# Attentions of a two-block model on one NeuronCore: maxima taken scaled and negated, scores issued one step further ahead

## What is computed

```python
s = jnp.einsum('bqhd,bkhd->bhqk', qb, k).astype(jnp.float32) * scale
s = jnp.where(key_pos[None, :] <= q_pos[:, None], s, -jnp.inf)
p = jax.nn.softmax(s, axis=-1)
if mix is not None:
    p = mix(p)                      # diff_branch: p of head 2h minus lam * p of head 2h+1
return jnp.einsum('bhqk,bkhd->bqhd', p.astype(v.dtype), v)
```

## Time and profile before

| | |
|---|---|
| median of 3 executions | 4144.8 us (4137.83 to 4156.16) |
| the profiled execution | 4138.23 us, its span 4136.4 us |
| busy, share of the span | PE 93%, PEld 78%, DVE 40%, ACT 35%, POOL 34% |
| granted TensorE clock, mean | 0.973 |

### The profile page before, as it was taken

The page is one execution under the profiler, slowest core; times in us unless marked ns, Lnnn a source line. Parts: engine busy times, 40 slices in busy tenths (PEclk is TensorE's granted clock), DMA queues, the critical chain, the costliest instruction groups (busy, mean ns, idle before and its releaser), DMA issues. The chain is left out here.

```text
span 4136.4 us, 57230 instructions
## 1 busy us (share of the span) xinstructions
PE 3854.7 (93%) x23428; PEld 3229.0 (78%) x23428; DVE 1670.0 (40%) x3370; ACT 1430.4 (35%) x2322; POOL 1414.1 (34%) x525
## 2 busy tenths in 40 slices
PE   6998989999989899999989989999999888889999
PEld 5766878887876678788769967888888777867887
DVE  5845152322384524332261464311124676754111
ACT  3434242342234423333232364211122544433221
POOL 2211323343321132234322322223222567643342
PEclk8899999999999999999999999999999999999999
DMA  3221414434222142344412211112222111103332
GB/s 116 56 83 40 139 54 141 122 118 127 76 56 83 39 130 64 120 119 142 127 51 72 75 25 32 51 52 76 62 57 71 43 42 52 41 17 88 91 98 74
DMA packets 476080, 323.18 MB, mean 78 GB/s; under 512 B 31449, under 2 KB 472236, under 8 KB 475820
## 3 DMA queue, kind: packets, MB, share of 16 engines
q1 hardware_dynamic: 422112, 268.18, 22.5%
q10 hardware_dynamic: 53708, 51.33, 3.7%
HBM read 315.74 MB, written 2.16 MB: 77 GB/s over the span
## 5 line engine op out<-in xcount | busy, mean ns | idle before, releaser
L96 POOL TENSOR_TENSOR w_lo<-w_raw,w_hi 128x2048 fp32r<-128x2048 f32 (+6 forms) x329 | 1157.5, 3523 | 2417.8 <-ACT w_hi L228 2417.4
L228 ACT ACTIVATE w_hi<-w_raw 128x2048 fp32r<-128x2048 f32 (+3 forms) x278 | 471.9, 1698 | 1113.8 <-PE psum L264 1068.2
L262 PE MATMUL psum<-xF_hi,w_hi 128*128 128x512 f32 x1232 | 493.3, 400 | 15.7 <-ACT a_relud L1673 6.8
L264 PE MATMUL psum<-xF_hi,w_lo 128*128 128x512 f32 x1232 | 484.3, 393 | 0.0
L263 PE MATMUL psum<-xF_lo,w_hi 128*128 128x512 f32 x1232 | 480.7, 390 | 0.0
L262 PE MATMUL psum<-ffn_h_hi,w_hi 128*128 128x512 f32 (+1 forms) x1056 | 376.5, 357 | 2.2 <-issue 1.3
L264 PE MATMUL psum<-ffn_h_hi,w_lo 128*128 128x512 f32 (+1 forms) x1056 | 375.0, 355 | 0.0
L263 PE MATMUL psum<-ffn_h_lo,w_hi 128*128 128x512 f32 (+1 forms) x1056 | 373.7, 354 | 0.0
L262 PEld LDWEIGHTS psum<-xF_hi,w_hi 128*128 128x128 f32 x1232 | 232.6, 189 | 69.9 <-ACT a_relud L1673 8.4
L264 PEld LDWEIGHTS psum<-xF_hi,w_lo 128*128 128x128 f32 x1232 | 232.1, 188 | 53.8
L263 PEld LDWEIGHTS psum<-xF_lo,w_hi 128*128 128x128 f32 x1232 | 232.2, 189 | 48.7
(11 more groups left out here) (554 smaller groups left out, 8183.4 us busy)
## 6 DMA issues: line engine op xcount, KB each, us to landing
w_raw<-in_w_in_dram SPq DMA_DIRECT2D x56, 1024.0 KB, 5.2
ada_w<-in_ada_w_dram ACTq DMA_DIRECT2D x48, 1024.0 KB, 6.9
w_raw<-in_ffn_w_in_dram SPq DMA_DIRECT2D x88, 512.0 KB, 5.1
w_raw<-in_w_in_dram SPq DMA_DIRECT2D x78, 512.0 KB, 4.2
w_raw<-in_ffn_w_out_dram SPq DMA_DIRECT2D x32, 704.0 KB, 4.6
w_raw<-in_w_branch_dram SPq DMA_DIRECT2D x74, 256.0 KB, 4.6
w_raw<-in_hg_w_in_dram SPq DMA_DIRECT2D x32, 512.0 KB, 4.8
w_raw<-in_na_w_qkv_dram SPq DMA_DIRECT2D x12, 1024.0 KB, 5.1
```

Of the source, the lines that this page charges most:

```text
L96: return eng.tensor_tensor(pair.lo, src, pair.hi.bitcast(F32), ALU.subtract)
L228: act.activation(self.w(j).hi, self.raw_w(j), ACT.Copy).then_inc(*self.high_done.up(1))
L262: pe.matmul(out, left.hi, right.hi, start=first, stop=False)
L264: return pe.matmul(out, left.lo, right.hi, start=False, stop=last)
```

## The change

H gives the scaled and negated maximum straight away: the fused operation multiplies by -scale and reduces with min, into `bias`, and writes the masked scores already multiplied by -scale; the exponential then takes `scale=-1.0`. The `tensor_scalar` behind it, its wait, and the tile `top` of `paired_attention` are gone. Without mask and with scale 1.0 (`na`) `tensor_reduce` runs with `negate=True`; `mem` keeps both operations. The exponential of a unit is released by its own unit, where it was released by the step.

In `attention` the loops are written anew: PE issues T(s-1), S(s+1), F(s-2); DVE issues H(s+1), R(s-2), I(s-1); ACT issues c(s-1), e(s+1), and `raise_part` after them. `paired_attention` keeps its order.

```diff
                 C.enter(pe)
+                scores(0)
                 for s in range(NU // 2 + 2):
-                    if s < NU // 2:
-                        scores(s)
                     turn(s - 1)
+                    if s + 1 < NU // 2:
+                        scores(s + 1)
                     if features:
                         feature_sums(s - 2)
...
                     if mask is None:
-                        step(dve.tensor_reduce(column(top, u), scores_at(u)[:, 0:N], AX.X, ALU.max))
+                        if scale == 1.0:
+                            dve.tensor_reduce(column(bias, u), scores_at(u)[:, 0:N], AX.X, ALU.max, negate=True).then_inc(*max_found.up(1))
+                        else:
+                            step(dve.tensor_reduce(column(top, u), scores_at(u)[:, 0:N], AX.X, ALU.max))
+                            dve.tensor_scalar(column(bias, u), column(top, u), -scale, None, ALU.mult).then_inc(*max_found.up(1))
                     else:
...
-                        step(dve.tensor_tensor_reduce(dst, src, mask, 1.0, -3.0e38, ALU.add, ALU.max, column(top, u)))
-                    if not features:
-                        dve.tensor_scalar(column(bias, u), column(top, u), -scale, None, ALU.mult).then_inc(*max_found.up(1))
-                    elif u % 2:
-                        dve.tensor_scalar(columns(bias, u // 2), columns(top, u // 2), -scale, None, ALU.mult).then_inc(*max_found.up(2))
+                        dve.tensor_tensor_reduce(dst, src, mask, -scale, 3.0e38, ALU.add, ALU.min,
+                                                 column(bias, u)).then_inc(*max_found.up(1))
...
                 C.enter(dve)
-                for s in range(NU // 2 + 2):
-                    for u in group(s):
+                for s in range(-1, NU // 2 + 2):
+                    for u in group(s - 1):
+                        if u in dve_copies:
+                            copy(u)
+                    for u in group(s + 1):
                         highest(u)
...
                 C.enter(act)
-                for s in range(NU // 2 + 1):
-                    for u in group(s):
-                        N = width(u)
...
+                for s in range(-1, NU // 2 + 1):
                     for u in group(s - 1):
...
+                    for u in group(s + 1):
+                        N = width(u)
+                        act.wait_ge(*max_found.at(u + 1))
+                        if u >= 4:
+                            act.wait_ge(*turned.at(u - 3))
+                        src, by = (scores_at(u)[:, 0:N], scale) if units[u]["mask"] is None else (probs[u % 4][:, 0:N], -1.0)
+                        act.activation(probs[u % 4][:, 0:N], src, ACT.Exp, bias=column(bias, u), scale=by,
+                                       accum_out=column(den, u)).then_inc(*exped.up(1))
```

`paired_attention` has the same edit of its fused operation and its exponential:

```diff
-                    step(dve.tensor_tensor_reduce(probs[:, u % 6, 0:N], scores_at(u)[:, 0:N], units[u]["mask"], 1.0, -3.0e38,
-                                                  ALU.add, ALU.max, column(top, u)))
-                    dve.tensor_scalar(column(bias, u), column(top, u), -scale, None, ALU.mult).then_inc(*max_found.up(1))
+                    dve.tensor_tensor_reduce(probs[:, u % 6, 0:N], scores_at(u)[:, 0:N], units[u]["mask"], -scale, 3.0e38,
+                                             ALU.add, ALU.min, column(bias, u)).then_inc(*max_found.up(1))
```

More of the change, by code:

```diff
@@ L885, in _ @@
                 C.enter(dve)
-                for s in range(NU // 2 + 2):
-                    for u in group(s):
+                for s in range(-1, NU // 2 + 2):
[3 more added lines that the diff above has]
+                    for u in group(s + 1):
                         highest(u)
                     if features:
-                        for u in group(s - 1):
-                            if u in dve_copies:
-                                copy(u)
                         if s >= 2:
@@ L907, in _ @@
                 C.enter(act)
-                for s in range(NU // 2 + 1):
-                    for u in group(s):
-                        N = width(u)
-                        act.wait_ge(*max_found.at(u + 1))
-                        if u >= 4:
-                            act.wait_ge(*turned.at(u - 3))
-                        src = scores_at(u)[:, 0:N] if units[u]["mask"] is None else probs[u % 4][:, 0:N]
-                        act.activation(probs[u % 4][:, 0:N], src, ACT.Exp, bias=column(bias, u), scale=scale,
-                                       accum_out=column(den, u)).then_inc(*exped.up(1))
+                for s in range(-1, NU // 2 + 1):
                     for u in group(s - 1):
@@ L952, in paired_attention @@
         probsT, probs = sb("probsT", [P, 2, 512]), sb("probs", [P, 6, 512])
-        top, bias, den, rec = (sb(n, [P, 8]) for n in ("top", "bias", "den", "rec"))
+        bias, den, rec = (sb(n, [P, 8]) for n in ("bias", "den", "rec"))
         share = sb("share", [P, 4])
@@ L1079, in _ @@
                             N = width(u)
-                            act.activation(probs[:, u % 6, 0:N], probs[:, u % 6, 0:N], ACT.Exp, bias=column(bias, u), scale=scale,
+                            act.activation(probs[:, u % 6, 0:N], probs[:, u % 6, 0:N], ACT.Exp, bias=column(bias, u), scale=-1.0,
                                            accum_out=column(den, u)).then_inc(*exped.up(1))
```

## The result

The changed kernel takes **4089.3 us** (median of 4 executions, 4086.2 to 4093.5) against 4145.5 for the one before beside it; the ratio is 0.9863, 95% interval 0.9839 to 0.9887. It is faster, and by more than forecast: the median moved by 56 us, where 42.4 were counted. Run twice more, the same kernel gave ratios of 0.9852 (0.9828 to 0.9876) and 0.9854 (0.9839 to 0.9869), so the size holds.

A forecast was written before the change was run, and what follows sets the result against it. PE, 93% busy, was taken as the bound, so only its idle time could be won. Terms of 35.0, 3.8 and 3.6 sum to 42.4: 4138.2 becomes 4095.8, plus 6.6 gives 4102 us; 8-in-10 range 4089 to 4123.

The forecast's parts named there:

- What bounds and what goes: In `attention`, PE, 93% busy, waits for ScalarE's copies before T; all these waits, 32.5 us in 41 pieces, should go.
- the hand-overs on PE: Changing between S, T and F in `attention`: three per step before and after, counted 0, from -11 to +11 us.
- rival (c): The fused operation with min and a factor takes twice its time, deciding in `diff`; kernel slower at 4167 us; chance 0.03.
- (a): In `na`, loading the bias tables becomes the bound, so its waits stay; 4122 us; chance 0.07.
- (b): In `attention`, equal PE waits appear elsewhere because DVE's order changed; half the copy-wait gain lost, 4120 us; chance 0.12.
- the cover named for it: In `attention`, T(s) and S(s+2) hide F's wait for I; without them it would cost 0.9 us a step.
- Third term: In `diff`, removing the TENSOR_SCALAR saves 0.17 us a step where DVE sets the pace: -3.6 us, between 0 and 6.4.
- The pacing: In `diff`, DVE sets the pace in about 21 of 32 steps; in each layer's first steps PE is the bound.
- First term: PE's waits for ScalarE's copies in `na`, `dsa`, `mla` and `mem` go: -35.0 us.
- rival (d): Slow-clock stretches at feature attentions' starts shift with shorter gaps, 5 us either way; chance 0.04 for more gain, with cheap hand-overs.
- Second term: At attention starts PE gets its first exponentials earlier, 0.61 us in `dsa` and `mla`, 1.01 in `na`: -3.8 us in all.
- The distance to the median: For the whole kernel, the median of the runs was assumed to stay 6.6 us above the profiled execution.

The follow-up runs named there:

- old_pe_order: The changed kernel with PE's old loop order S(s), T(s-1), F(s-2) in `attention`, DVE and ScalarE streams as changed; ratio to before 1.0135.
- diff_only: The kernel before with only the edit of `paired_attention` (fused maximum scaled and negated, tensor_scalar and its wait gone); ratio to before 0.9967.
- arith_only: The kernel before with only the new arithmetic in `attention`, exponentials released by their own unit, old order and `diff` kept; ratio to before 0.9909.
- columns_only: The kernel before with the tensor_scalar of `dsa`, `mla`, `na` on one column per unit, releasing that unit's exponential; ratio to before 0.9935.
- order_only: The kernel before with only the new loop order in `attention`, the tensor_scalar behind the maxima kept; ratio to before 0.9908.
- order_columns: The kernel before with the new order, old arithmetic, and the tensor_scalar of `dsa`, `mla`, `na` on one column per unit; ratio to before 0.9907.

## Why the prediction was right and wrong

**What bounds and what goes: right.** `na` moved by the 20.7 us counted for it, all copy waits went, the hand-overs on PE cost nothing in `na` (a wide turn of S, T and F without a wait takes 3.33 in both orders). In `mla`, where a turn of S and T with N = 512 and an F of 384 without any wait took 3.81 in the old order and 3.76 in the new, they were 0.05 cheaper, inside the bound of 0.1. The fused operation with min and a factor takes what it took (0.68 at 512, mean 486 ns in both kernels): rival (c) is out. Rivals (a) and (b) did not come; old_pe_order shows that (b) was a real edge, and that the cover named for it is what holds it off. In `dsa` the -15.0 against 12.7 counted is in part the luck of two profiles: in the mean (two profiles of the old code, six with the changed `attention`) it is -13.4.

**Third term, wrong: -3.6 counted with 6.4 at most, -11 measured** (diff_only -10.5, after -11.2 and, run again, -9.9; the 0.4 that the second term counts in `diff` are in these). The step that failed is the row taken as the distance "without one between them": the 0.74 of the earlier trace rows. Nothing stood between those two maxima but a wait (`step`), and the wait was itself part of what the change removes. Without either the distance is 0.61. The rule cited there, that a semaphore costs nothing extra, made the row look like a floor; the text said that "the row cannot tell the two apart", and should then have left the bound open below 0.74. The pacing was right for steps of N = 384 and 512 and the last of 256 (some 20 of 32 are 0.42 shorter), and the narrow ones gain less.

**First term in `mla`: -4.0 counted, -11.0 measured.** The waits fell by 2.1 and 1.8 us, as counted. In the mean the stages differ by 3.7 and 6.0 us (two profiles of the old code, six with the changed `attention`). The rest is rival (d), which had been sized at 5 us for all stages, and PE work that got shorter. The low stretch was 7.3 to 14.0 us in eight `mla` stages with PE's old order (before, diff_only, arith_only, columns_only; 34.7 and 13.8 in old_pe_order) and 3.8 to 7.0 in the sixteen with the new one and no added matmuls; the 7.3 and the 7.0 are equal within their error. Over these 24 stages without old_pe_order, PE's time without its idle time grows by 0.41 (old order) and 0.44 us (new) for each us that it works at 1.2 GHz, and with none of that it would be 45.4 and 44.1 us. PE's work at the low clock fell from 7.6 and 13.3 to 6.8 and 6.6 us in the mean. So the two layers come out as

| us | first layer | second layer |
|---|---|---|
| waits | 2.1 | 1.8 |
| low clock | 0.4 | 2.9 |
| PE's work itself | 1.2 | 1.3 |

Of the last row the cheaper hand-over is some 0.7 (16 steps of 0.05); the other half has no cause that a run shows.

Rival (d) had the sign of its larger case and not the reason. It put the shorter stretch down to the shorter gap at the start. arith_only shortened that gap (PE's first wait, 1.8 and 2.0 us where before has 2.4 and 2.6) and kept the long stretch; order_only left it at 2.4 and 2.6 and had the short one. So it goes with the order, but for the one stage with 7.3 (diff_only), and how was not taken apart.

**Second term: right.** PE's wait for the first exponentials fell by 0.6 in each layer of `dsa` and `mla` (2.9 to 2.3, 2.6 to 2.0, 2.4 to 1.8, 2.6 to 2.0) and by 1.0 in `na` (3.5 to 2.5), as counted.

**The distance to the median: not where it failed.** The prediction added the 6.6 us between the median and the profiled execution of before, and after's profiled execution is 0.5 above its median. But with this distance the forecast is the old median less 42.4, and the median moved by 56 as the attentions did (59 in the two profiles). The miss of 14 us stands in the attentions: some 7 in `diff`, 7 in `mla`, 2 in `dsa`, less the scatter of the rest. Measured between the two profiled executions the miss looks like 6 us, and that is luck: the spans between the attentions came out 10.6 longer.

**What the sum hides.** The parts overlap. Alone they give 38, 38 and 14 us by their ratios to 4146 (0.9908, 0.9909, 0.9967), 90 together, and the change gives 57 to 61.

## What to carry to other kernels

Ask of each row used as a floor what else stands in it: two instructions with a wait between them are no measure of two without. A release that comes once for two units can cost more than the instructions it saves; release each by its own. Where two edits aim at one wait, work out each alone first, and move the streams of two engines only together.

## What the runs showed of the hardware that I had not expected

- A wait of DVE for its own last operation is worth 0.11 to 0.12 us behind a fused maximum, more than a small instruction costs there without a wait (0.07).
- A TENSOR_SCALAR of 128x2 in SBUF took up to 1.35 us while GpSimd worked, one of 128x1 0.15 us (order_only, order_columns). The holds of `na` in order_only add up to 9.0 us, and `na` lost only some 1.4 by them.
- The granted clock in `mla` stayed at 2.4 GHz (1.00) with three added matmuls, where without them 6.9 us ran at 1.2 GHz; the stage gained 1.3 to 1.5 us of it. A us of PE work at 1.2 GHz costs the stage 0.41 to 0.44 us.
- The untouched 3630 us of the program scatter by 16 us from profile to profile, as much as a third of this change.
